# Head scores of an attention-style mixer: two heads at a time in two PSUM banks, a third bank, and the modulation sums moved

## The reference, cut to what matters

```
A  mLSTM matrix memory       s = (q k^T) * exp(d_log - m_t)
B  forgetting attention      s = q k^T * scale + (F_q - F_k), causal softmax
C  stick-breaking attention  z = q k^T * scale, log-space cumulative sums
D  native sparse attention   selected and window branch: softmax(q k^T * scale + bias), and a compressed branch
```

## Time and profile before

| | us |
|---|---|
| median of 3 runs | 1579.16 |
| profiled execution, its own time | 1575.83 |
| its span, first to last instruction | 1574.0 |
| layer 0: slots to the last output tile | 90.36 to 248 |
| layer 0: dense SwiGLU | 252 to 490 |
| layer 1: slots to the last output tile | 539.9 to 684 |
| layer 1: experts | 700 to 1574 |
| TensorE busy | 1466.0 (93%) |
| VectorE busy | 471.2 (30%) |
| mean granted TensorE clock | 0.975 of full |

### The profile page before, as it was taken

The page is one execution under the profiler, slowest core; times in us unless marked ns, Lnnn a source line. Parts: engine busy times, 40 slices in busy tenths (PEclk is TensorE's granted clock), DMA queues, the critical chain, the costliest instruction groups (busy, mean ns, idle before and its releaser), DMA issues.

```text
span 1574.0 us, 16822 instructions
## 1 busy us (share of the span) xinstructions
PE 1466.0 (93%) x6928; PEld 720.5 (46%) x6928; DVE 471.2 (30%) x937; ACT 197.6 (13%) x427; POOL 2.5 (0%) x23
## 2 busy tenths in 40 slices
PE   6899999999999999988989999999999999987886
PEld 2576755555544756662424333434343344332322
DVE  4478725344334555352100111112110110110001
ACT  1123223000003132330000000100000001000000
POOL 0000000000000000000000000000000000000000
PEclk9999989999999999989999999999999999999999
DMA  9935535887874310039999999999999999999995
GB/s 345 360 136 182 187 112 197 270 299 247 310 280 151 108 55 1 1 115 409 419 414 419 408 417 404 411 411 419 411 418 409 413 409 410 411 409 418 418 401 225
DMA packets 151647, 481.60 MB, mean 306 GB/s; under 512 B 15848, under 2 KB 33640, under 8 KB 144144
## 3 DMA queue, kind: packets, MB, share of 16 engines
q1 hardware_dynamic: 150120, 478.64, 78.4%
q10 hardware_dynamic: 1448, 1.84, 0.4%
HBM read 479.41 MB, written 1.06 MB: 305 GB/s over the span
## 4 chain that ended last, share of the span: by engine, by line
PE 77%; DMA 17%; DVE 2%; SPq 1%; ACT 1%; issue 1%; DVEq 0%; ACTq 0%
PE bank L1560 23%; PE bank L1596 14%; DMA ring<-in_moe_wu 13%; PE bank L1432 9%; PE bank L1190 7%; PE bank L1450 5%; PE bank L1179 4%; PE bank L1397 3%; DMA ring<-in_moe_wg 2%; DMA ring<-in_ada_w 1%; PE bank L1317 1%; PE bank L1169 1%; SPq L772 1%; PE bank L1267 1%; PE bank L1266 1%
## 5 line engine op out<-in xcount | busy, mean ns | idle before, releaser
L1560 PE MATMUL bank<-ring,h_T 128*32 128x512 f32 (+1 forms) x2240 | 310.2, 614 | 47.4 <-DMA ring<-in_moe_wu 35.3
L1596 PE MATMUL bank<-ring,m_qk_T 128*32 128x512 f32 (+2 forms) x1344 | 246.7, 596 | 12.6 <-issue 10.0
L1560 PEld LDWEIGHTS bank<-ring,h_T 128*32 128x32 f32 (+1 forms) x2240 | 99.8, 118 | 244.5 <-issue 243.4
L1560 PE MATMUL bank<-ring,cmp_region 128*128 128x512 f32 x448 | 196.3, 592 | 1.2 <-DVE m_s_region L2289 1.2
L1596 PEld LDWEIGHTS bank<-ring,m_qk_T 128*32 128x32 f32 (+2 forms) x1344 | 88.6, 128 | 166.4 <-issue 166.4
L1432 PE MATMUL bank<-ring,h_T 128*128 128x384 f32 (+1 forms) x448 | 156.8, 503 | 0.7 <-DVE m_s_region L2088 0.7
L1560 PEld LDWEIGHTS bank<-ring,cmp_region 128*128 128x128 f32 x448 | 84.0, 190 | 102.0 <-issue 102.0
L1190 PE MATMUL bank<-ring,h_T 128*128 128x512 f32 (+1 forms) x320 | 119.1, 522 | 0.8 <-ACT wide L879 0.5
L1432 PEld LDWEIGHTS bank<-ring,h_T 128*128 128x128 f32 x448 | 83.3, 190 | 61.3 <-issue 15.5
L1026 ACT ACTIVATE m_qk_T<-bank 128x512 f32<-128x512 f32 x35 | 20.9, 597 | 656.4 <-PE bank L1576 655.9
L2289 DVE SCALAR_TENSOR_TENSOR m_s_region<-m_s_region,bank 128x512 f32<-128x512 f32 x35 | 24.1, 688 | 262.1 <-PE bank L1560 262.1
(11 more groups left out here) (355 smaller groups left out, 1041.5 us busy)
## 6 DMA issues: line engine op xcount, KB each, us to landing
ring<-in_moe_wg SPq DMA_DIRECT2D x56, 2048.0 KB, 21.2
ring<-in_moe_wu SPq DMA_DIRECT2D x56, 2048.0 KB, 21.2
ring<-in_moe_wd SPq DMA_DIRECT2D x54, 2048.0 KB, 23.1
ring<-in_ada_w SPq DMA_DIRECT2D x28, 1024.0 KB, 8.8
ring<-in_ada_w SPq DMA_DIRECT2D x10, 2048.0 KB, 14.2
ring<-in_w_in SPq DMA_DIRECT2D x10, 2048.0 KB, 10.7
ring<-in_ffn_wg SPq DMA_DIRECT2D x6, 1536.0 KB, 10.2
ring<-in_ffn_wu SPq DMA_DIRECT2D x6, 1536.0 KB, 9.0
```

The lines of the kernel that those rows point to most:

```text
L1560: last = mm(b[c0:c1, :], xT[st.team % 2][:, k, c0:c1], w, start=k == 0, stop=k == KC - 1)
L1596: last = mm(ps[half][c0:c1, :], hbT[:, unit, 128 * q + c0:128 * q + c1], down_at(slot, 512)[:, q, 512 * half:512 * half + 512], start=st.b ...
```

## The change

The scores of heads i and i+1 (i even, of the kinds sel, win, mlstm and fox) are now made together in slot i (`first_two`), with matmuls of the even and of the odd head in turn, each into its own bank; odd slots have no `first`. A third bank (3) joins banks 0 and 1 for heads 0 to 15; stick heads stay single. mlstm's matmul for the minima is a step of its own (`minima`) in each slot. `negf` is written twice, on partitions 0 to 7 and 64 to 71, so that the odd fox head's additions use the upper rows. Because bank 3 now serves heads, chunks 5 to 9 of the modulation and the router's constant use bank 2, with new waits, and the sums lie in other slots (`SUMS_IN_SLOT`): chunk 6 is reduced in slot 12 (was 10), 7 in 14 (was 12), 8 in 16 (was 15), 9 in 17 (was 16).

```diff
+PAIRED = HEADS.index(("stick", 0))
+HEAD_BANK = [(0, 3, 1)[i % 3] if i < PAIRED else (1, 0)[i % 2] for i in range(NH)]
-SUMS_IN_SLOT = (0, 0, 0, 1, 2, 0, 2, 2, 2, 1, 1, 2, 2, 0, 2, 3, 0, 0, 0, 0, 0, 0)
+SUMS_IN_SLOT = (0, 0, 0, 1, 2, 0, 2, 2, 1, 1, 0, 1, 2, 2, 2, 2, 2, 0, 0, 0, 0, 0)
...
         if s < NH:
-            pe("first", s)
+            if s >= PAIRED:
+                pe("first", s)
+            elif s % 2 == 0:
+                pe("first_two", s)
+            if HEADS[s][0] == "mlstm":
+                pe("minima", s)
...
-        negf = sb("neg_cum_logf", [8, S])
+        negf = sb("neg_cum_logf", [DH + 8, S])
...
         def ada_bank(l, c):
-            return ps[6 + c % 2] if (l, c // 4) == (0, 0) else ps[3] if (l == 0) == (c < 10) else ps[7]
+            return ps[6 + c % 2] if (l, c // 4) == (0, 0) else ps[2] if l == 0 and 5 <= c < 10 else ps[3] if (l == 0) == (c < 10) else ps[7]
...
                 if lin >= 4:
                     pe.wait_ge(mod_evac, lin)
+                if lin == 5:
+                    pe.wait_ge(cmp_taken, 1)
+                elif lin == 6:
+                    pe.wait_ge(fox_T_evac, 2)
...
+                def bank_free(i):
+                    before = [j for j in range(i) if HEAD_BANK[j] == HEAD_BANK[i]]
+                    if not before:
+                        if HEAD_BANK[i] == 3:
+                            pe.wait_ge(mod_evac, (5, 24)[l])
+                    elif HEADS[before[-1]][0] == "stick":
+                        pe.wait_ge(stick_shift, N_STICK * l + HEADS[before[-1]][1] + 1)
+                    else:
+                        pe.wait_ge(head_pT, N_P * l + count(PKINDS, before[-1]))
...
+                def first_two(i):
+                    kind, h = HEADS[i]
+                    two = (i, i + 1)
+                    for n in two:
+                        bank_free(n)
...
+                    fox = kind == "fox"
+                    ops = [operands(n) for n in two]
+                    cuts = (slice(0, ops[0][0][1].shape[-1]), slice(ops[0][0][1].shape[-1], 384))
+                    for part, c in enumerate(cuts):
+                        for n, op in zip(two, ops):
+                            last = mm(ps[HEAD_BANK[n]][:, c], *op[part], start=part == 0, stop=bool(part) and not fox, skip_group_check=True)
+                            if part and kind in ("sel", "win"):
+                                last.then_inc(head_scores, 1)
+                    if fox:
+                        for part, c in enumerate(cuts):
+                            for n in two:
+                                p0 = DH * (n % 2)
+                                sel = ident[p0:p0 + 8, p0 + H + HEADS[n][1]:p0 + H + HEADS[n][1] + 1].to_broadcast([8, 128])
+                                last = mm(ps[HEAD_BANK[n]][:, c], sel, negf[p0:p0 + 8, 0:c.stop - c.start], start=False, stop=bool(part), skip_group_check=True)
+                                if part:
+                                    last.then_inc(head_scores, 1)
+                def minima(i):
+                    h = HEADS[i][1]
+                    if h == 0:
+                        pe.wait_ge(cmp_taken, l + 1)
+                        if l == 0:
+                            pe.wait_ge(mod_evac, 6)
+                        else:
+                            pe.wait_ge(router_bias_in, 1)
                     else:
+                        pe.wait_ge(head_shift, N_P * l + count(PKINDS, i - 1))
+                    mm(ps[2][:, 0:256], ident[0:H, h:h + 1].to_broadcast([H, 128]), negm[:, :],
+                       start=True, stop=True).then_inc(head_scores, 1)
...
-                            pe.wait_ge(mod_evac, (10, 24)[l])
+                            pe.wait_ge(head_pT, N_P * l + count(PKINDS, PAIRED - 3))
...
-                    do(TS(negf[:, :], cumf[:, :], -1.0, None, ALU.mult))
+                    for p0 in (0, DH):
+                        do(TS(negf[p0:p0 + 8, :], cumf[:, :], -1.0, None, ALU.mult))
```

More of the change, by code:

```diff
@@ L620, in program @@
         router_done = sem("router_done")
+        router_bias_in = sem("router_bias_in")
         router_shift = sem("router_shift")
@@ L1227, in fox_transposes, with operands @@
                     last.then_inc(fox_T, 1)
-                def first(i):
-                    kind, h = HEADS[i]
[L1232 to L1237, removed]
+                def bank_free(i):
[7 more added lines that the diff above has]
+                        pe.wait_ge(head_pT, N_P * l + count(PKINDS, before[-1]))
+                def operands(i):
+                    kind, h = HEADS[i]
+                    r = slice(DH * (h % 2), DH * (h % 2) + DH)
+                    if kind in ("mlstm", "stick"):
+                        T_ = mqkT if kind == "mlstm" else sT
+                        q, k = T_[r, h // 2, :], T_[r, 2 + h // 2, :]
+                        return (k[:, 0:128], q), (k[:, 128:256], q[:, 128:256])
+                    if kind == "fox":
+                        q, k = fT[r, h // 2, :], fT[r, 2 + h // 2, :]
+                    else:
+                        q, k = nT[r, h // 2, :], nT[r, 2 + ((h % 2) ^ (kind == "win")), :]
+                    return (q[:, 0:128], k[:, 0:128]), (q[:, 128:256], k)
+                def first(i):
+                    if HEADS[i][1] == 0:
+                        pe.wait_ge(proj_evac, NG * (l + 1))
+                    bank_free(i)
+                    (a, b), (c, d) = operands(i)
+                    n = b.shape[-1]
+                    mm(ps[HEAD_BANK[i]][:, 0:n], a, b, start=True, stop=False, skip_group_check=True)
+                    mm(ps[HEAD_BANK[i]][:, n:384], c, d, start=False, stop=True, skip_group_check=True).then_inc(head_scores, 1)
+                def first_two(i):
+                    kind, h = HEADS[i]
+                    two = (i, i + 1)
+                    for n in two:
+                        bank_free(n)
                     if h == 0 and kind == "sel":
@@ L1241, in first @@
                         pe.wait_ge(mqk_ready, l + 1)
-                        pe.wait_ge(cmp_taken, l + 1)
-                    elif kind == "mlstm":
-                        pe.wait_ge(head_shift, N_P * l + count(PKINDS, i - 1))
                     elif h == 0 and kind == "fox":
                         pe.wait_ge(fox_T_evac, 2 * (l + 1))
[L1247 to L1258, removed]
-                    else:
[L1260 to L1268, removed]
-                            sel = ident[0:8, H + h:H + h + 1].to_broadcast([8, 128])
-                            mm(b[:, 0:128], sel, negf[:, 0:128], start=False, stop=True, skip_group_check=True)
-                            last = mm(b[:, 128:384], sel, negf[:, :], start=False, stop=True, skip_group_check=True)
@@ L1405, in router_constant @@
                     pe.wait_ge(mod_evac, 24)
+                    pe.wait_ge(cmp_taken, 2)
                     for k in range(KC):
-                        last = mm(ps[3][:, 0:N_EXP], modc[:, 24 + k:25 + k].to_broadcast([128, 128]), rw[:, k, :], start=k == 0, stop=k == KC - 1)
+                        last = mm(ps[2][:, 0:N_EXP], modc[:, 24 + k:25 + k].to_broadcast([128, 128]), rw[:, k, :], start=k == 0, stop=k == KC - 1)
                     last.then_inc(router_done, 1)
@@ L1411, in mixer @@
                         "nsa_T": nsa_transposes, "kv_T": kv_transposes, "cmp_scores": compressed_scores, "cmp_turn": cmp_turn,
-                        "cmp_out": cmp_product, "fox_T": fox_transposes, "first": first, "second": second, "third": third,
+                        "cmp_out": cmp_product, "fox_T": fox_transposes, "first": first, "first_two": first_two, "minima": minima, "second": second, "third": third,
                         "mix_T": mix_transposes, "wout": wout}
```

14 lines of the change are left out of this document (8 added, 6 removed).

## The result

The changed kernel took 1569.6 us (median of four executions, 1567.7 to 1570.5) where the kernel before, beside it on the same chip, took 1578.6: a ratio of 0.994, 95% interval 0.9923 to 0.9958, so 9 us faster. The forecast was 1565.6, in a range of 1560 to 1575. The profiled execution took 1570.17 us (span 1568.4), against 1575.83 (span 1574.0) before; between these two the difference is only 5.7 us.

The account below looks back on a forecast made before the run. TensorE was taken to bound both mixers, with VectorE limiting layer 0's gain. Layer 1's 9.3, layer 0's 1.4 and the clock's 2.9 sum to 13.6 us: 1579.2 - 13.6 = 1565.6 us, range 1560 to 1575.

Parts of the forecast that it names:

- Both ends of the bounds: Sel pair's scores on TensorE: 0.84 us if everything overlaps, which the forecast took, 1.5 us if nothing does.
- the 0.18 us beyond six units: One head's scores: 0.84 us, six units making 0.66, the other 0.18 spent entering and leaving the 64-row form.
- Rivals 1 and 2: Pair's scores: half overlap, kernel at 1569 us, chance 0.10 (1); no overlap, 1576.5 us, chance 0.08 (2).
- the reading of rows 8 against the cited rule: Four tiles' 64 records in 7.11 us taken as full overlap, against the skill's strict program order (pair 1.06 us).
- 9.3 us forecast: Layer 1's heads: gain of 9.3 us, with 0.4 us of waiting kept in slot 1.
- waits of 0.4 and 0.6 us in slots 1 and 5: Layer 0, slots 0 to 11: the only waits counted there, 0.4 us in slot 1 and 0.6 in slot 5.
- those before heads 13 and 15: Layer 0, slots 12 and 14: TensorE waits 2.2 and 2.5 us for VectorE, which has the moved sums.
- The one before head 14 (2.1): Layer 0, slot 13: two sums follow `finish(2)` on VectorE, so TensorE waits 2.1 us.
- the 1.7 us in slots 16 and 17: Layer 0: estimated waits of some 1.7 us, from chunk 9's sums before the first stick head's copy.
- 1.4 net: Layer 0 without the clock: 1.7 us left after the new waits, less 0.3 for `negf`, a gain of 1.4 us.
- three stretches like the first: Layer 0's slow clock: three stretches costing 5.0 us instead of 7.9 lost before, so 2.9 us back.
- rival 3: VectorE's waits in layer 0's slots 13 to 17 lower the clock more; layer 0 loses 3.5, kernel 1573.4 us; chance 0.14.

Follow-up runs that it names:

- no_turns: Changed kernel with all of the even head's matmuls in each pair issued before the odd head's, no alternation: 1566.2 us, run once.
- l1_only: Changed kernel with pairs and third bank in layer 1 only, layer 0 as before the change: 1563.3 us, ratio 0.9929.
- filled: Changed kernel with two unread 512-column matmuls before the transposes of each of heads 13 and 15 in layer 0: 1567.1 us, ratio 0.9927.
- early3: Changed kernel with layer 0's reductions of chunks 6, 7, 8 earlier in slots 12, 14, 16, and 3, 1, 1, 3, 2 sums in slots 12 to 16: 1560.4 us.
- few_sums_after: Changed kernel without six of eight sum instructions for each of chunks 5 to 9: layer 0 9.7 us shorter than the kernel before with the same cut.
- early2: Changed kernel with layer 0's reductions of chunks 6, 7, 8 earlier in slots 12, 14, 16, and one sum moved from slot 13 to 12: 1562.2 us.
- wide_sums: early3 with layer 0's chunks 6 to 9 each reduced by one 512-column product, not eight one-column records: layer 0's heads 2.6 us shorter than early3's.

## Why the prediction was right, and where it was not

**The pair: right.** Both ends of the bounds were measured, 0.86 us with full overlap (forecast 0.84), 1.50 on the same rows (1.5). Of the 0.18 us beyond six units, 0.10 lies at the entry: the pair's first two records last 0.213 us to the next start, the next two, of the same width, 0.112. Rivals 1 and 2 are out, and the reading of rows 8 against the cited rule held (`no_turns`).

**Layer 1: right.** 9.3 us forecast, 9.3 measured in `l1_only` at equal low time. In the changed kernel 7.7 us arrived: 3.4 us more at the low clock take 1.7. That its low time would stay at 3.4 was assumed without a word.

**The moved sums: right in mechanism, too heavy in amount.** Of the waits of 0.4 and 0.6 us in slots 1 and 5 there is none in slot 1, 0.22 in slot 5 and 0.46 in slot 6 (117.22 and 122.33); those before heads 13 and 15, forecast as 2.2 and 2.5, as 2.63 and 2.58. The one before head 14 (2.1) and the 1.7 us in slots 16 and 17 did not show as waits, because TensorE did those slots at half clock and was the later one; in `filled`, where head 14's slot is at full clock, 1.76 us of the first are there. At full clock layer 0 went from 145.09 to 140.64, 4.4 us, where the forecast had 1.4 net. Part of these 4.4 us is such waits, hidden by the slow clock.

**The failed term: "three stretches like the first", 2.9 us back from the clock in layer 0.** It was 30.7 us low against 17.1: 6.8 us lost. The forecast had named the waits as what lets the clock fall and then given three stretches of the shortest kind; they were 6.8, 6.8 and 17.1 us, the last two behind the waits of 2.6 us. The -6.8 of the clock and the 4.4 above are one split of the measured -2.4, not two checks of it. This is rival 3, whose layer 0 (-3.5) is nearer to the profile than the forecast's +4.3; in the total the two are equally near, 1573.4 and 1565.6 against 1569.6. That the total still fell close to the forecast is luck: the median is 9 us better, but the profiled executions differ by only 5.7 (7.7 from layer 1, -2.4 from layer 0, 0.3 from the rest) of the 13.6 forecast. The profiled execution of the kernel before was 2.8 us below the median of the runs beside the changed one, and 1.7 us came back in the dense part, where before had 3.4 us low and after none, of which the forecast says nothing. I had added the 3.3 us between profile and median to the forecast as a fixed offset; after the change the profiled execution lies at its own median (1570.2 and 1569.6).

**`negf`, banks, loads: nothing to be seen.** TensorE waits 0.9 us before the second fox transposes and 1.0 us before the fox pair in both kernels; dense work follows the heads without a wait on weights. The forecast had the first dense up weights about 4 us earlier; they were issued at 189.47, 2.0 us later than before, with 57 us of cover left, so the error cost nothing.

**What stays open.** Why the clock falls at 158.5 us in `early3` and not in `few_sums_after`, whose TensorE does the same instructions from 145 to 158 us, each start within 0.1 us of the other's. Of what was changed only VectorE's load differs there. Why one sum moved by a slot (`early2`) goes with 10 us more at the low clock. And why the low time of the unchanged layer 0 was 17.1 us in one execution and 10.2 in another, while the changed kernel's came out alike twice.

## What to carry to other kernels

Score products of two heads with 64 rows each cost as much together as one, provided they lie on different halves of the rows; in both orders of issue tried here it was the same. Each head also wrote a bank of its own in every version, so whether one bank would do is not shown. Before spending time that such a change frees on TensorE, look at what the engine that feeds it has queued: here 22.5 us of VectorE's sums decided whether layer 0 gained 9.7 us or lost 2.4. Three reductions issued ahead of the rest of their slot, with two sums shifted by a slot, gave 8.6 us; what the shifted sums add is within the noise. Where the clock falls and waits stand side by side, neither can be added up alone: the slow clock hides waits, which come back when the clock does.

## What the hardware showed that I had not expected

- Records of two row halves issued as a whole head and then the other still started two by two, 13 ns apart; in `no_turns` the second head's first record started beside the first head's first, ahead of three records issued before it.
- Eight records of one column take as long as one product of 512 columns (0.87 us in `early3`, 0.91 in `wide_sums`, at full clock), but the version with them behind short matmuls had 20.5 us low and the other 6.8, in one execution of each.
- With two dense products of no use in each of two waits, 17.1 us were low instead of 30.7, again in one execution of each kind, and the kernel was not measurably faster.
- The three low stretches of the changed kernel's layer 0 came again in a second execution, at the same places to 0.4 us and with the same 30.7 us in all.
